# Expert weights in 2 MB halves with an order fixed beforehand, and a reordered router stretch, in an encoder layer with 32 experts

## The reference, cut to what matters

```
x  = x + gt1 * (merged @ w_o)                       # residual x1
h2 = rmsnorm(x, norm2_g) * (1 + sc2) + sh2
router: top-1 group of 4, then top-2 of its 8 experts (32 experts)
y  = (silu(h2 @ w1[e]) * (h2 @ w3[e])) @ w2[e]      # w1, w3: 2048x512, w2: 512x2048
x  = x + gt2 * sum(weight * y)
out = rmsnorm(x, final_g)
```

## Time and profile before

| | us |
|---|---|
| runs | 1783.74 median of 3 (1783.24 to 1787.66) |
| the profiled execution, its own time | 1783.57 |
| span of the profiled execution | 1781.8 |
| TensorE busy | 1702.7 (96%) |
| VectorE busy | 970.7 (54%) |
| ScalarE busy | 427.7 (24%) |
| read from HBM | 639.2 MB, 360 GB/s over the span |

### The profile page before, as it was taken

The page is one execution under the profiler, slowest core; times in us unless marked ns, Lnnn a source line. Parts: engine busy times, 40 slices in busy tenths (PEclk is TensorE's granted clock), DMA queues, the critical chain, the costliest instruction groups (busy, mean ns, idle before and its releaser), DMA issues.

```text
span 1781.8 us, 26191 instructions
## 1 busy us (share of the span) xinstructions
PE 1702.7 (96%) x10198; PEld 998.9 (56%) x10198; DVE 970.7 (54%) x1199; ACT 427.7 (24%) x534; POOL 0.9 (0%) x5
## 2 busy tenths in 40 slices
PE   4999999999999999999999999999999999999986
PEld 3888567777777776875444444444444444444442
DVE  5564959867778678566353443434343434343434
ACT  3001034433333233443121212121212121111111
POOL 0000000000000000000000000000000000000000
PEclk9999999999999999999999999999999999999998
DMA  9998538889879697835999999999999999999995
GB/s 369 387 385 323 189 142 336 334 311 352 331 287 361 259 367 317 308 131 211 414 423 425 423 425 423 425 423 425 424 425 424 424 424 425 423 425 424 425 424 241
DMA packets 128239, 641.95 MB, mean 360 GB/s; under 512 B 8003, under 2 KB 8131, under 8 KB 76099
## 3 DMA queue, kind: packets, MB, share of 16 engines
q1 hardware_dynamic: 127762, 639.18, 89.3%
q0 software_dynamic: 144, 1.70, 0.2%
q10 hardware_dynamic: 290, 0.46, 0.1%
HBM read 639.21 MB, written 2.10 MB: 360 GB/s over the span
## 4 chain that ended last, share of the span: by engine, by line
PE 60%; DMA 35%; DVE 2%; SPq 1%; issue 1%; DVEq 0%; ACT 0%
DMA ring<-in_exp_w 33%; PE ps L954 11%; PE ps L699 7%; PE ps L701 7%; PE ps L700 7%; PE ps L604 6%; PE ps L661 5%; PE ps L908 3%; PE ps L617 3%; DMA ring<-in_ada_w 2%; PE ps L772 2%; PE ps L773 2%; PE ps L774 2%; PE ps L886 1%; DVE r_m L1380 1%
## 5 line engine op out<-in xcount | busy, mean ns | idle before, releaser
L954 PE MATMUL ps<-ring 128*64 128x512 f32 x1968 | 448.4, 597 | 24.5 <-DMA ring<-in_exp_w 24.5
L954 PEld LDWEIGHTS ps<-ring 128*64 128x64 f32 x1968 | 145.9, 136 | 287.3 <-issue 287.2
L1762 DVE SCALAR_TENSOR_TENSOR r_h<-ps,stat,r_h 128x1024 f32<-128x1024 f32 x124 | 153.4, 1279 | 141.8 <-PE ps L935 141.8
L1721 DVE TENSOR_TENSOR r_c<-ps,scale 128x512 f32<-128x512 f32 x64 | 44.3, 692 | 305.4 <-PE ps L886 298.5
L700 PE MATMUL ps<-g_lo,h_hi 128*128 128x512 f32 x512 | 199.3, 389 | 0.0
L699 PE MATMUL ps<-mix_hi,h_hi 128*128 128x512 f32 x384 | 156.5, 408 | 0.0
L1155 ACT ACTIVATE mix_hi<-ring 128x1024 fp32r<-128x1024 f32 x96 | 101.5, 1061 | 222.3 <-PE ps L701 222.3
L701 PE MATMUL ps<-mix_hi,h_lo 128*128 128x512 f32 x384 | 149.6, 390 | 0.0
L1294 ACT ACTIVATE y_hi<-ring 128x512 fp32r<-128x512 f32 x62 | 38.1, 631 | 444.1 <-DVE ring L1749 444.1
L604 PE MATMUL ps<-r_h,ring 128*128 128x256 f32 x640 | 141.1, 383 | 1.3 <-ACT r_h L1106 1.3
L1472 DVE SCALAR_TENSOR_TENSOR r_m<-ring,col,r_m 128x2048 f32<-128x2048 f32 x53 | 124.4, 2347 | 31.8 <-DMA ring<-in_ada_w 31.8
(11 more groups left out here) (280 smaller groups left out, 1768.8 us busy)
## 6 DMA issues: line engine op xcount, KB each, us to landing
ring<-in_exp_w SPq DMA_DIRECT2D x254, 1024.0 KB, 23.2
ring<-in_ada_w SPq DMA_DIRECT2D x78, 1024.0 KB, 8.3
ring<-in_w_in SPq DMA_DIRECT2D x36, 2048.0 KB, 10.1
ring<-in_exp_w SPq DMA_DIRECT2D x32, 2048.0 KB, 24.3
r_b<-in_exp_w SPq DMA_DIRECT2D x32, 2048.0 KB, 25.3
ring<-in_w_in SPq DMA_DIRECT2D x20, 1024.0 KB, 14.2
r_b<-in_ada_w SPq DMA_DIRECT2D x18, 1024.0 KB, 9.9
ring<-in_w_o SPq DMA_DIRECT2D x8, 2048.0 KB, 8.3
```

Of the source, the lines that this page charges most:

```text
L954: last = mm(ps[m * NWIN:(m + 1) * NWIN, 2, :], xe[:, k, :], w[:, kk * F:(kk + 1) * F], start=(k == 0), stop=(k == KT - 1))
L1762: V.scalar_tensor_tensor(out=x1n, in0=ps[:, (6, 4)[t]:(6, 4)[t] + 2, :].rearrange("p b n -> p (b n)"), scalar=tok_w[:, t:t + 1], in1=x1n, ...
```

## The change

- The up weights of an expert come as four loads of 2 MB (w1 and w3 of half c), a row of 16 KB on each partition. `w13_used` rises once a half. Expert 0 takes slots 0, 1, 2 and `r_m`; later experts take slots 3, 0, 1, 2.
- Passes 0 to 15 are the first windows of experts 0 to 15, then come further windows (none for these inputs), then the first windows of experts 16 to 31. The first half of the loads needs no table. Each engine's loop is now three loops. Expert 1's first load is issued before the router is done. The table tells where the first windows stand by a third small product and a constant (`K_LATE`).
- TensorE does the up products half by half: half 0, all of `second`, the next gather, half 1 with two combines after its first quarter and two at its end. The last pass loads its half 1 in four pieces of 1 MB, and its w2 in four.
- The `gt2` row is laid out in the first pass, after half 0. Its copy on ScalarE moves along.
- Router stretch: the last four `w_o` pieces go 28, 30, 29, 31, and the last products n outer, t inner, starting when piece 30 is there. The additions to x1 follow that order. VectorE copies the transposed banks of t = 0 only, ScalarE those of t = 1. Roots and inverses for both t come together, and ScalarE makes the diagonals. The high part is written in halves. The products with the counts come ahead of the rests of t = 1, and these use banks 4 to 7.
- Head: piece 3 of each part and piece 0 of the first are loaded in four DMAs by k. ScalarE copies part 0's two banks instead of VectorE.
- Tail: combines, additions, squares and means go t by t.

```diff
@@ SP
+            def load_w13(p, e, i, landed):
+                w, c = (e1_v, e3_v)[i % 2], i // 2
+                sp.dma_start(w13_slot(p, i).rearrange("p (k n) -> p k n", k=8),
+                             w[bass.ds(e, 1), :, c, :, :].rearrange("e p j n -> (e p) j n")).then_inc(landed[i], 16)
+            for i in range(3):
+                sp.wait_ge(g_used, 128 + 4 * (5 + i))
+                load_w13(0, 0, i, first_in)
             sp.wait_ge(wo_done, 8)
-            load_w13(0, 3)
+            load_w13(1, 1, 0, w13_in)
             sp.wait_ge(logitT_done, 2)
...
+            load_w13(0, 0, 3, first_in)
+            sp.wait_ge(w13_used, 2 + 1)
+            load_w13(1, 1, 1, w13_in)
+            load_w13(1, 1, 2, w13_in)
+            sp.wait_ge(w13_used, 2 + 2)
+            load_w13(1, 1, 3, w13_in)
+            def load_front(p, e, prior):
+                sp.wait_ge(w13_used, 2 * p + 1)
+                for i in range(2):
+                    load_w13(1, e, i, w13_in)
+                for h in range(2):
+                    sp.wait_ge(w2_used, 4 * p + 2 * h + 2)
+                    load_w2(prior, h)
+                sp.wait_ge(w13_used, 2 * p + 2)
+            def load_pass(p, e, prior):
+                load_front(p, e, prior)
+                for i in range(2, 4):
+                    load_w13(1, e, i, w13_in)
+            with sp.Fori(2, EARLY) as p:
+                load_pass(p, p, p - 1)
             sp.wait_ge(table_ready, 1)
...
@@ TensorE
+            def whole_pass(p, is_last=False):
+                pe.wait_ge(xe_ready, 2 * p + 1)
+                gather(1, sel_e)
+                turn(p)
+                turn_windows(p)
+                for m in range(2):
+                    pe.wait_ge(w13_in[m], 16 * p)
+                first_half(1, 0, range(8)).then_inc(w13_used, 1)
+                second(p, 0, 4)
+                if not is_last:
+                    gather_next(p)
+                pe.wait_ge(xe_ready, 2 * p + 2)
...
+                first_half(1, 1, range(4))
+                for i in range(2):
+                    combine(p, i)
...
+                first_half(1, 1, range(4, 8)).then_inc(w13_used, 1)
+                for i in range(2, 4):
+                    combine(p, i)
...
-            pe.wait_ge(g_lo_done, 128 + 32)
-            for t in range(TT):
-                for n in range(4):
+            for n in range(4):
+                pe.wait_ge(g_lo_done, 128 + (30 if n < 2 else 32))
+                for t in range(TT):
                     for k in (14, 15):
                         last = wo_products(k, t, n)
                     last.then_inc(wo_done, 1)
...
@@ ScalarE
             square(0, 0)
+            square(1, 0)
+            copy_turned(0)
+            copy_turned(1)
             square(0, 1)
+            copy_turned(2)
+            square(1, 1)
+            copy_turned(3)
             root(0)
-            square(1, 0)
+            root(1)
             part_high(0)
-            square(1, 1)
-            root(1)
             part_high(1)
```

More of the change, by code:

```diff
@@ L186, in used, with ada_count @@
             return HEAD * part + ORDER[part].index(n) + 1
+        def ada_count(i):
+            return 32 * sum(j % ADA_FIRST == i % ADA_FIRST and j % 4 != 3 and j > 0 for j in range(i + 1))
         def head_w(i):
@@ L221, in build @@
         ada_in = [sem(f"ada_in{i}") for i in range(ADA_FIRST)]
+        ada_first = [sem(f"ada_first{i}") for i in range(4)]
+        ada_last = [sem(f"ada_last{i}") for i in range(4)]
         part_added = sem("part_added")
@@ L297, in build @@
         wT_ready = sem("wT_ready")
-        w13_in = [sem(f"w13_in{i}") for i in range(CHUNKS)]
+        w13_in = [sem(f"w13_in{i}") for i in range(4)]
         w2_in = [sem(f"w2_in{i}") for i in range(2)]
@@ L391, in load_head @@
                     sp.wait_ge(sq_done, 2)
+                if piece == 3 or i == 0:
+                    for kk in range(4):
+                        sp.dma_start(head_ada(i)[:, kk, :, :],
+                                     ada_v[:, 4 * piece + kk, 0:2 * D].rearrange("p (v n) -> p v n", v=2)
+                                     [:, :, part * PART:(part + 1) * PART]
+                                     ).then_inc((ada_last if i else ada_first)[kk], 16)
+                    return
                 for v in range(2):
@@ new lines, in _ @@
+            with sp.Fori(EARLY, NE - 1) as e:
+                p = e + more
+                prior = sp.value_load(etab[0:1, bass.ds(p - 1, 1)], min_val=0, max_val=NE - 1)
+                load_pass(p, e, prior)
+            load_front(end_p, NE - 1, NE - 2)
+            for j in range(2):
+                for m, w in enumerate((e1_v, e3_v)):
+                    sp.dma_start(w13_slot(1, 2 + m)[:, j * 2048:(j + 1) * 2048].rearrange("p (k n) -> p k n", k=4),
+                                 w[NE - 1, :, 1, 4 * j:4 * j + 4, :]).then_inc(last13_in[2 * j + m], 16)
@@ L831, in _ @@
                     last.then_inc(logitT_done, 1)
+            for n in range(4):
+                for t in range(TT):
+                    turn_x1(n, t)
+            pe.wait_ge(rw_scaled, 1)
+            for n in range(4):
+                if n == 2:
+                    mm(ps[:, 5, 0:36], ones, cst_k[:, :], start=True, stop=False)
+                    mm(ps[:, 5, 0:36], ones[0:1, :], lrow[0:1, :], start=False, stop=True).then_inc(cst_done, 1)
+                for t in range(TT):
+                    logit_part(n, t)
             def logits(t):
@@ L1030, in _ @@
             gather(1, sel)
-            first(0, False)
+            first_pass()
+            with pe.Fori(1, EARLY) as p:
+                whole_pass(p)
             pe.wait_ge(table_ready, 1)
@@ L1107, in _ @@
                   scale=scale1[:, k:k + 1]).then_inc(h_ready, 1)
+                if k == 3:
+                    for n in (3, 4):
+                        act.wait_ge(head_used, used(0, n))
+                        A(late[:, n - 3, :], ps[:, 6:8, :].rearrange("p b n -> p (b n)"), ACT.Copy
+                          ).then_inc(part_added, 1)
             act.wait_ge(head_used, used(3, 0))
```

450 lines of the change are left out of this document (217 added, 233 removed).

## The result

The changed kernel takes 1816.54 us (median of 4 runs, 1814.61 to 1817.15); the kernel before took 1783.96 us beside it (4 runs, 1783.24 to 1787.66). The ratio is 1.0177, with a 95% interval of 1.0164 to 1.019. The forecast was 1769 with a range of 1763 to 1782, so the sign was wrong and the time lies 34 us above the range. The profiled execution took 1817.05 us, with a span of 1815.2.

A forecast was written before the change was run, and what follows sets the result against it. DMA engines were taken as the bound during the passes, 3% ahead of TensorE. Faster streaming and an earlier router end the last down products 14.4 us sooner: 1783.57 - 14.4 = 1769; range 1763 to 1776, to 1782 with the slow-rate case.

The forecast's parts named there:

- the part on the passes: Expert passes: TensorE's work unchanged at 28.8 us a pass, under the DMAs' 29.33 by 0.5, with fewer waits.
- second rival: Passes: TensorE becomes the bound, deciding from 28.93 us a pass; chance 0.10 for 29.1 to 29.5, 0.06 above.
- P: TensorE's own time for one expert pass, read as 28.8 us.
- The rate: Weight streaming: rows of 16 KB raise the DMA rate from 424 to 429 GB/s, an expert taking 29.33 us; the largest term.
- first rival: Weight streaming: the rate stays at 424 GB/s, last weights land 10.3 us later, result 1779.5 us; chance 0.17.
- The first up product: End of the router stretch: starts at 825.1 us instead of 829.68, 4.55 us earlier with w_o gap and head.
- The empty queue: DMA restart after the router: no loads queued for some 5 us until pass 1's half 0 is used; full from 853.8.
- The gain at the end: Last pass: last down products over at 1751.9 us instead of 1766.34, 14.4 us earlier.
- The w_o gap: Before TensorE's last eight banks: pieces 28 and 30 first remove a 2.4 us wait, -2.4 us.
- the head: Kernel start: one VectorE copy less and split loads win TensorE's waits, -0.7 us (0 to -1).

The follow-up runs named there:

- the probe: Separate program without the layer, only TensorE products at varied weight column steps: 31 ns a product at 2 and 4 bytes, 35 at 8, 62 at 16.
- the kernel with groups of four: Changed kernel with parts stored in groups of four columns, weight columns 8 bytes apart, rows still 16 KB: 1776.55 us, ratio 0.9951 to the kernel before.
- the kernel without the middle loop: Second of three loops left out, here of the changed kernel with columns in groups of four: 1774.76 us, ratio 0.9947; of the changed kernel itself: 1808.0 us.
- the kernel with parts side by side: Changed kernel with ScalarE writing the parts so that a weight load's 128 columns are neighbours, in scattered writes: 1816.98 us, ratio 1.0177 to the kernel before.

## Why the prediction was wrong

**The step that failed** is the sentence in the part on the passes: "Its products, gathers and combines are the same." Products and combines are, the gathers are not: 2 x 1.3 us a pass. The number of instructions and their shapes are the same, and I took their durations from the earlier trace rows without asking how far apart their operands lie. The row assignment changes that distance from 8 to 16 bytes, and the probe and the kernel before with the new assignment alone show that this is enough.

The prediction's second rival, TensorE as the bound, named what happened and gave another reason for it (a half that waits for both its matrices). It decides at P = 28.93; P is 30.12. By its own formula the last pass would start at 842.7 + 3.4 + 30 x 30.12 = 1749.7. It started at 1758.3: pass 0 ended 4.4 us later, at 847.14 (the first up product 2.1 later, its half 8.20 for 7.02 with a granted clock of 0.66 from 825 to 830, a gather 1.3 longer), and the handover took 7.6 instead of 3.4. I had put 0.06 on P above 29.6, since I only looked for waits that could lengthen a pass. That it named the right bound comes from the two engines being close; the gathers were not in it.

SBUF has lines of 16 bytes, and accesses that leave the line each time pay for it, at least two hits a line being needed, says the Trainium skill (SBUF — State Buffer, Door 1: The DMA port swizzle); its free stride of 8 bfloat16 or 4 float32 would make the change's 16 bytes free. The probe agrees with the two hits (35 ns at 8 bytes, 62 at 16) and not with that list: for both types a step of exactly 16 bytes costs double. The skill also puts a limit of 8 bytes on GpSimd's reads, with half as much again above it (GPSIMD Engine Reference, Performance pitfalls for Q7 kernels). No run here shows GpSimd; TensorE's limit lies between 8 and 16 bytes as well, and it pays twice. The two hits or the 8 bytes should have made me ask; the list alone would have called the step free.

**P, TensorE's own pass, was mis-sized**: 28.8 by 29.68 less the waits of the earlier trace rows, 27.5 by the kernels with the 16-byte step, where nothing else delays it. The waits for weights as the profile names them are not all of the slack: in the earlier trace rows TensorE counts as busy for 766.7 of 800 us, 28.4 a pass, 0.9 more than it needs where nothing holds it up. How the slack comes to count as busy time was not followed. With 28.8 the second rival seemed to decide 0.13 us away; with 27.5 it was 1.4 away, and the 2.6 us of the gathers crossed that and went 1.2 beyond, which over 30 passes is 36 us.

**The rate: right.** Rows of 16 KB flow at 428 to 429 GB/s over 290 us (in the four kernels that the DMAs bind with such rows), rows of 8 KB at 424 over the same stretch, both before and in the changed kernel with rows of 8 KB. In time, 1.0007 less 0.9951 of 1784 is 10.0 us; the prediction's first rival was 10.3 above its forecast.

**The first up product: right**, where the gathers are fast: 824.76 for 825.1. In the changed kernel it came at 827.18; the two gathers ahead of it are 1.3 us longer each. Turning began at 796.7 and ended at 800.9 in the changed kernel, for 797.1 and 801.0; its last banks did wait for an addition, but 0.2 us only, since VectorE began its additions at 788.5, after the last low part. The empty queue came too: in the kernel with groups of four half 0 of pass 1 ended at 852.28 for 852.2, and the DMA share is 0.88 from 840 to 850 us and 0.67 from 850 to 860, together some 4.5 us without work.

**The gain at the end: too large by 8.4 us** even with fast gathers (last down products over at 1760.3 for 1751.9), by the chain with groups of four. Half 1 of pass 9 landed at 1091.61, where the forecast's end less 21 passes gives 1088.6: 3.0 somewhere between the filling of the queue and there, not followed further. A pass is 29.37 for 29.33: 0.8 over 21. From there to pass 30's landing at 1710.29 (1710.42 less 0.13) another 2.0 are missing, which the window of 1290 to 1300 shows as a dip to 344 GB/s: the handover, which I had covered with the queue. Without the middle loop the dip is gone. The last pass began 0.6 sooner after it than in my sum. In it, VectorE's additions and windows stand between the last combines (1745.02) and the last products (1750.37), so that this stretch is 2.2 longer; and the last products took 9.9 instead of 8.9, partly at half clock (next section). 3.0 + 0.8 + 2.0 - 0.6 + 2.2 + 1.0 = 8.4. The last term has to do with the clock and not with the change: the same 32 products take 7.1 us at full clock in the kernel without the middle loop, and the 8.8 that I took from the earlier trace rows had the lower clock in it too (0.71 over their first 5.9 us).

**The w_o gap and the head**, small terms, went as forecast together: by TensorE's records turning began at 796.72 for 800.05 before, 3.3 us for 3.1, and the wait of 2.4 us is gone. They were not tried one by one. Nor was the fixed order without the halves.

## What to carry to other kernels

Where a change renumbers rows or columns, write down for each engine that reads or writes them how many bytes lie between neighbours, before and after; an unchanged instruction count says nothing about it. Keep the step between the columns of TensorE's weights at 8 bytes or less. For the other operands the runs show only that steps of 32 and 256 bytes are dear, so a step above 8 bytes is worth a trial there. When a layout must change, store runs of neighbours that fill 8 bytes, as the kernel with groups of four does, so that neither writer nor reader has a wide step. And where two engines are within 5% of each other, find the second one's true pace from a kernel in which it is the bound, since subtracting its named waits gave 1.3 us a pass too much here.

## What the runs showed of the hardware that was not expected

- The step of TensorE's weight loads: 31 ns a product at 2 and 4 bytes, 35 at 8, 62 at 16, 63 at 32 and 64 at 64. The moving operand in float32: 604 ns for 512 columns in neighbours or groups of 16 bytes, 1097 at 32 bytes. In bfloat16: 379 ns for neighbours, 1029 at 256 bytes (in the kernel with parts side by side, at both levels of the clock).
- ScalarE's scattered writes are far dearer than scattered reads: 2786 ns for 512 elements at 256 bytes against 592; reading 1024 float32 at 32 bytes took 2120 against 1133.
- Leaving a loop with seven skipped turns and entering the next stopped TensorE for 6.24 us (3.39 us for leaving with eight skips; 0.8 and 0.7 us without the middle loop), and the clock was lower after it. Windows of the changed kernel:

```profile
1300.00:1304.00 4.00, 0.00 (x0) 0.00 (x0) 0.96 (x1) 0.00 (x0) 0.00 (x0) 1.00 1.00 424
1304.00:1308.00 4.00, 2.86 (x45) 2.81 (x46) 1.29 (x5) 0.00 (x0) 0.00 (x0) 0.50 1.02 430
1308.00:1312.00 4.00, 4.00 (x23) 2.16 (x23) 1.73 (x3) 1.08 (x3) 0.00 (x0) 0.65 0.74 307
1312.00:1316.00 4.00, 4.00 (x22) 1.39 (x20) 0.00 (x0) 0.00 (x0) 0.00 (x0) 1.00 0.01 4
```

The clock is granted at half, 1.2 GHz, until it returns to 2.4 GHz within the third window, and the stop costs 7.6 us instead of 6.2. The same is seen in the last products with groups of four: VectorE's work holds TensorE up from 1745.7 to 1750.4, and 1749.3 to 1756.1 us shows a granted clock of 0.50. It doesn't always follow: without the middle loop TensorE is held up in the same way from 1743.2 to 1747.8, the clock stays at 1.00, and the products take 7.1 us for 9.9. Over the nine profiled executions these products take 7.1 us in three, 8.8 in two and 9.8 to 10.0 in four, and what decides it was not found. In the fourth window the queue is empty because TensorE has freed no slot for so long; here the stop of one engine becomes a stop of the other.
